# Block sums of the FFN up-projection: built per pair in SBUF instead of ahead in DRAM

## The reference

```python
def conv_ffn(h, p):
    u = dwconv(h @ p['w_up'], p['ffn_conv']) + p['ffn_conv_b']
    val, gate = jnp.split(u, 2, axis=-1)
    return (val * jax.nn.silu(gate)) @ p['w_down']
...
        h2 = rmsnorm_2(h_res, g_ffn_pre[l])
        up = centred_dwconv(h2 @ w_up[l], conv_w_ffn[l], conv_b_ffn[l])
        a, v = jnp.split(up, 2, axis=-1)
        ffn_out = (jax.nn.gelu(a) * v) @ w_down[l]
        h_res = h_res + rmsnorm_2(ffn_out, g_ffn_post[l])
```

## Time and profile before

| | |
|---|---|
| three runs | 3824.38, 3827.13, 3827.26 us, median 3827.13 |
| profiled execution, and its span | 3828.93 us, 3827.1 us |
| PE, PE weight loads busy | 3424.5 (89%), 3114.0 (81%) |
| DVE, ACT, POOL busy | 2276.1 (59%), 1580.3 (41%), 234.1 (6%) |
| DMA queues: q1 (SP and others), q0 (POOL) | 332.72 MB, 28.5%; 191.47 MB, 17.2% |

### The profile page before, as it was taken

The page is one execution under the profiler, slowest core; times in us unless marked ns, Lnnn a source line. Parts: engine busy times, 40 slices in busy tenths (PEclk is TensorE's granted clock), DMA queues, the critical chain, the costliest instruction groups (busy, mean ns, idle before and its releaser), DMA issues.

```text
span 3827.1 us, 72929 instructions
## 1 busy us (share of the span) xinstructions
PE 3424.5 (89%) x30711; PEld 3114.0 (81%) x30711; DVE 2276.1 (59%) x3617; ACT 1580.3 (41%) x2735; POOL 234.1 (6%) x399
## 2 busy tenths in 40 slices
PE   8999978867798989889999996499999999999999
PEld 4787778867787778667788996379999989999999
DVE  5477756756575764776776883122223577777576
ACT  4566633333234764533344552111113443334454
POOL 2000000000000000000000112100000000000110
PEclk9999989888898999999999998699999999999999
DMA  6244455457523305333345766961113333344675
GB/s 234 74 143 136 142 201 185 162 126 175 136 64 77 80 29 145 97 108 110 114 136 186 264 214 232 253 133 38 45 50 91 117 103 111 108 140 122 240 243 163
DMA packets 396766, 528.85 MB, mean 138 GB/s; under 512 B 20596, under 2 KB 311895, under 8 KB 392345
## 3 DMA queue, kind: packets, MB, share of 16 engines
q1 hardware_dynamic: 353160, 332.72, 28.5%
q0 software_dynamic: 43280, 191.47, 17.2%
HBM read 441.17 MB, written 175.21 MB: 161 GB/s over the span
## 4 chain that ended last, share of the span: by engine, by line
PE 45%; DVE 6%; issue 3%; DMA 3%; ACT 2%; another core or an unknown queue 2%; DVEq 2%; ACTq 0%; POOL 0%
PE psum L3587 8%; PE psum L3588 7%; PE psum L3589 7%; PE psum L2849 4%; PE psum L2850 4%; PE psum L2851 4%; PE psum L2370 3%; PE psum L2372 3%; PE psum L2371 3%; DMA down_w_raw<-in_w_down 1%; DMA down_w_raw<-in_w_in 1%; DVE mix_u_val L3877 1%; DVE mix_u_gate L3877 1%; PE psum L3488 1%
## 5 line engine op out<-in xcount | busy, mean ns | idle before, releaser
L2236 DVE TENSOR_TENSOR down_w_lo<-down_w_raw,down_w_hi 128x1024 fp32r<-128x1024 f32 x228 | 270.5, 1187 | 562.2 <-ACT down_w_hi L2210 559.9
L2210 ACT ACTIVATE down_w_hi<-down_w_raw 128x1024 fp32r<-128x1024 f32 x228 | 234.7, 1029 | 695.5 <-PE psum L2851 283.5
L3434 DVE TENSOR_TENSOR mix_w_split<-mix_w_raw,mix_w_split 128x512 fp32r<-128x512 f32 x372 | 255.4, 688 | 296.1 <-ACT mix_w_split L3430 295.8
L2370 PE MATMUL psum<-down_ghi,down_w_hi 128*128 128x256 f32 x1408 | 404.1, 287 | 11.7 <-DVE down_glo L2241 11.5
L2372 PE MATMUL psum<-down_glo,down_w_hi 128*128 128x256 f32 x1408 | 399.5, 284 | 0.0
L2371 PE MATMUL psum<-down_ghi,down_w_lo 128*128 128x256 f32 x1408 | 399.2, 284 | 0.0
L3587 PE MATMUL psum<-mix_t_hi,mix_w_split 128*128 128x258 f32 (+1 forms) x1056 | 339.9, 322 | 13.7 <-DVE mix_t_lo L3815 13.6
L3588 PE MATMUL psum<-mix_t_hi,mix_w_split 128*128 128x258 f32 (+1 forms) x1056 | 339.3, 321 | 0.0
L3589 PE MATMUL psum<-mix_t_lo,mix_w_split 128*128 128x258 f32 (+1 forms) x1056 | 339.0, 321 | 0.0
L2849 PE MATMUL psum<-h_hi,down_w_hi 128*128 128x348 f32 (+2 forms) x768 | 254.1, 331 | 74.1 <-DVE down_w_lo L2236 35.8
L3430 ACT ACTIVATE mix_w_split<-mix_w_raw 128x512 fp32r<-128x512 f32 x372 | 228.0, 624 | 155.7 <-PE psum L3589 134.4
(11 more groups left out here) (499 smaller groups left out, 8537.1 us busy)
## 6 DMA issues: line engine op xcount, KB each, us to landing
down_w_raw<-in_w_down SPq DMA_DIRECT2D x176, 512.0 KB, 4.3
up_sums<-in_w_up POOLq DMA_DIRECT2D x48, 1408.0 KB, 20.1
mix_w_raw<-up_sums SPq DMA_DIRECT2D x176, 256.0 KB, 2.9
mix_w_raw<-in_w_up SPq DMA_DIRECT2D x132, 256.0 KB, 3.1
up_sums<-up_sums POOLq DMA_DIRECT2D x16, 1408.0 KB, 24.6
g_scratch<-mix_u_val POOLq DMA_DIRECT2D x44, 512.0 KB, 3.6
down_w_raw<-in_w_in SPq DMA_DIRECT2D x36, 512.0 KB, 4.0
down_g_part<-g_scratch POOLq DMA_DIRECT2D x6, 2816.0 KB, 16.6
```

The costliest lines, as they stand in the source:

```text
L2210: self.nc.scalar.activation(self.hi[s][:, 0:w], self.raw[s][:, 0:w], ACT.Copy).then_inc(self.w_high, 1)
L2236: last = self.nc.vector.tensor_tensor(self.lo[s][:, 0:w], self.raw[s][:, 0:w], self.hi[s][:, 0:w].bitcast(F32), ALU.subtract)
L2370: nc.tensor.matmul(out, w_hi[:, w], g_hi[:, :], start=(n == 0 and c % 2 == 0), stop=False, skip_group_check=True)
L3434: nc.vector.tensor_tensor(ring[s % 4][:, 1, :], raw[s % RAWS][:, :], ring[s % 4][:, 0, :].bitcast(F32), ALU.subtract).then_inc(w_low.sem, 1)
```

## The change

`sum_weights`, its calls and the tensor `up_sums` are gone. SP loads 5 tiles per pair in the late steps (A11, S1, S3, A12, A22, where S1 and S3 start as their first block). POOL adds the second block into each of S1 and S3 by an accumulating transfer from `w_up` into the SBUF tile (`add_blocks`, L3489 in the new numbering), two pairs ahead; its rows are 512 bytes. DVE makes the other two sums in place: `first_sum` adds S1 to A11 (for P6, L3471), and a second add puts A11 on A12 (for P3, L3463). ACT's high parts of P6 and P3 wait for these adds. In the order of steps, P3 of an early pair changes places with P1 of the pair behind it, where that pair is not early (7 times in each mixer). The norms' chain of the first half (a = 0) takes the form that the second half had, both run a step sooner, and one more `low_turns` stands ahead of the late steps.

```diff
-                sum_weights(pool, k, 0, i)
...
-        for i in range(32):
-            sum_weights(pool, self.k, 1, i)
...
+    for at in range(len(late) - 1):
+        if late[at][0] == "P3" and late[at][1] in EARLY and late[at + 1][0] == "P1":
+            late[at:at + 2] = late[at + 1], late[at]
...
+    tiles += [(what, i, "late") for i in range(KF) for what in ("A11", "S1", "S3", "A12", "A22")]
+    SOURCE = {"P1": "A11", "P6": "A11", "P7": "S3", "P5": "S1", "P2": "A12", "P3": "A12", "P4": "A22"}
...
+        if kind == "P6":
+            act.wait_ge(*w_added.at(2 * i + 1))
+        elif kind == "P3":
+            act.wait_ge(*w_added.at(2 * i + 2))
...
     def weight_low(dve, s):
...
+        if s + 1 < STEPS and steps[s + 1][0] == "P6":
+            first_sum(dve, steps[s + 1][1])
+        elif kind == ("P5" if i in EARLY else "P2") and s >= first_late:
+            dve.drain()
+            a11, a12 = (raw[tile_of[what, i, "late"] % RAWS] for what in ("A11", "A12"))
+            wait_landed(dve, tile_of["A12", i, "late"])
+            nc.vector.tensor_tensor(a12[:, :], a12[:, :], a11[:, :], ALU.add).then_inc(w_added.sem, 1)
+
+    def first_sum(dve, i):
+        t11, ts1 = tile_of["A11", i, "late"], tile_of["S1", i, "late"]
+        wait_landed(dve, t11)
+        wait_landed(dve, ts1)
+        dve.drain()
+        a11, s1 = raw[t11 % RAWS], raw[ts1 % RAWS]
+        nc.vector.tensor_tensor(a11[:, :], a11[:, :], s1[:, :], ALU.add).then_inc(w_added.sem, 1)
...
+    def add_blocks(pool, i):
+        for what, added in (("S1", "A22"), ("S3", "A11")):
+            t = tile_of[what, i, "late"]
+            slot = t % RAWS
+            pool.wait_ge(*w_landed[slot].at(landed_at(t)))
+            pool.dma_start(raw[slot][:, :].rearrange("p (k n) -> p k n", n=P), block(added, i),
+                           accum_op=ALU.add).then_inc(blocks_added[i % 2].sem, 16)
...
         def chain(a, e):
             if e == 1:
                 means(a, 0)
-            elif a == 1:
-                if 3 <= e <= 6:
-                    residual(a, 2 * e - 6, 2 * e - 5)
-                elif e == 8:
-                    means(a, 1)
...
+            elif 2 <= e <= 5:
+                residual(a, 2 * e - 4, 2 * e - 3)
+            elif e == 7:
                 means(a, 1)
```

More of the change, by code:

```diff
@@ L3321, in mixer_out_to_ffn @@
     w_up = spec["w_up"].rearrange("(k p) n -> p k n", p=P)
-    w_sums = [k.up_sums[spec["mixer"]][j].rearrange("(k p) n -> p k n", p=P) for j in range(4)]
     UNITS = 2 * KD
@@ L3329, in mixer_out_to_ffn @@
     first_late = 2 * UNITS + 2 * QUEUE
-    late_at = {i: min(s for s in range(first_late, STEPS) if steps[s][1] == i) for i in range(KF)}
+    late_at = {i: index["P3", i - 1] + 1 if i else first_late for i in range(KF)}
     RAWS = 10
-    landed_at = lambda s: 16 * (s // RAWS) + 16
+    tiles = [(*st, "all") for st in steps[:2 * UNITS]] + [(*steps[s], "early") for s in range(2 * UNITS, first_late)]
+    tiles += [(what, i, "late") for i in range(KF) for what in ("A11", "S1", "S3", "A12", "A22")]
+    TILES = len(tiles)
+    tile_of = {tile: t for t, tile in enumerate(tiles)}
+    landed_at = lambda t: 16 * (t // RAWS + 1)
+    SOURCE = {"P1": "A11", "P6": "A11", "P7": "S3", "P5": "S1", "P2": "A12", "P3": "A12", "P4": "A22"}
     chain_of = lambda s: (s // (2 * KD) - 1, s % (2 * KD)) if 2 * KD <= s < 6 * KD else (None, None)
@@ L3410, in mixer_out_to_ffn, with source, block, tile @@
     up.first_took = max(u[1] for u in upper if u[0] == "took")
-    up.raw_free = [max(s + 1 for s in range(STEPS) if s % RAWS // 2 == j) for j in range(2)]
     after.up = up
-    def source(s):
-        kind, i = steps[s][0:2]
-        if kind == "O":
-            h = steps[s][2]
-            return w_out[:, 4 * h:4 * h + 4, i % KD * P:i % KD * P + P]
-        if kind in SUMS:
-            return w_sums[SUMS.index(kind)][:, :, i * P:i * P + P]
-        c = (i + side[0 if kind == "P4" else 1]) * P
-        return w_up[:, 0:4, c:c + P] if kind == "P1" else w_up[:, 4:8, c:c + P]
-    def weight_high(act, s):
-        act.wait_ge(*w_landed[s % RAWS].at(landed_at(s)))
+    def source(t):
+        what, i = tiles[t][0:2]
+        if what == "O":
+            h = tiles[t][2]
+            return w_out[:, 4 * h:4 * h + 4, i % KD * P:i % KD * P + P]
+        return block(what, i)
+    def block(what, i):
+        low, c = {"A11": (0, 1), "P1": (0, 1), "A12": (4, 1), "P2": (4, 1), "A22": (4, 0), "S1": (0, 0), "S3": (0, 0)}[what]
+        c = (i + side[c]) * P
+        return w_up[:, low:low + 4, c:c + P]
+    def tile(s):
+        kind, i = steps[s][0:2]
+        return s if s < first_late else tile_of[SOURCE[kind], i, "late"]
+    def wait_released(eng, t):
+        what, i = tiles[t][0:2]
+        if t < first_late:
+            eng.wait_ge(*w_low.at(t + 1))
+        elif what == "A11":
+            eng.wait_ge(*w_added.at(2 * i + 2))
+        else:
+            eng.wait_ge(*w_low.at(index[{"S1": "P5", "S3": "P7", "A12": "P3", "A22": "P4"}[what], i] + 1))
+    def wait_raw(eng, j):
+        for slot in (2 * j, 2 * j + 1):
+            wait_released(eng, max(range(slot, TILES, RAWS)))
+    def wait_landed(eng, t):
+        what, i = tiles[t][0:2]
+        if what in BY_DMA:
+            eng.wait_ge(*blocks_added[i % 2].at(32 * (i // 2 + 1)))
+        else:
+            eng.wait_ge(*w_landed[t % RAWS].at(landed_at(t)))
+    up.wait_raw = wait_raw
+    def weight_high(act, s):
+        kind, i = steps[s][0:2]
+        t = tile(s)
+        if kind == "P6":
+            act.wait_ge(*w_added.at(2 * i + 1))
+        elif kind == "P3":
+            act.wait_ge(*w_added.at(2 * i + 2))
+        else:
+            wait_landed(act, t)
         if s >= 4:
@@ L3435, in weight_low @@
                                 ALU.subtract).then_inc(w_low.sem, 1)
-    def sync(sp):
-        for s in range(STEPS):
-            if s >= RAWS:
-                sp.wait_ge(*w_low.at(s - RAWS + 1))
-            elif before and s < 4:
-                sp.wait_ge(before.low, before.total - 1 + s // 2)
+        if s + 1 < STEPS and steps[s + 1][0] == "P6":
[5 more added lines that the diff above has]
+            nc.vector.tensor_tensor(a12[:, :], a12[:, :], a11[:, :], ALU.add).then_inc(w_added.sem, 1)
@@ new lines, in first_sum @@
+    def first_sum(dve, i):
[5 more added lines that the diff above has]
+        nc.vector.tensor_tensor(a11[:, :], a11[:, :], s1[:, :], ALU.add).then_inc(w_added.sem, 1)
+    def sync(sp):
+        for t in range(TILES):
+            if t >= RAWS:
+                wait_released(sp, t - RAWS)
+            elif before and t < 4:
+                sp.wait_ge(before.low, before.total - 1 + t // 2)
@@ L3466, in gpsimd @@
             pool.wait_ge(*x_stored[a].at(16 * KD))
+        for i in range(2):
+            add_blocks(pool, i)
         for m in range(KF):
+            if m + 2 < KF:
+                add_blocks(pool, m + 2)
             pool.wait_ge(*g_ready.at(m + 1))
@@ L3927, in vector @@
                 chain(a, e)
[L3928 to L3929 removed]
+            if first_late <= s < first_late + 3:
+                low_turns(TURNS[2 + s - first_late])
             if s >= first_late:
```

128 lines of the change are left out of this document (38 added, 90 removed).

## The result

The changed kernel takes 3635.4 us (median of four runs, 3630.13 to 3644.34) against 3827.2 us before: the ratio is 0.950, with a 95% interval of 0.948 to 0.952. The forecast was 3642. The total came out nearly as the sum said, but two of its three terms were wrong, in opposite directions: the scan gave 41 us more than forecast, the mixers cost 23 us more. That the total is within 7 us is luck in part.

What follows compares the result with a forecast made beforehand. Bounds: the sums' DMA traffic delaying loads in scan and merge stage; PE, with DVE short of slack, in the mixers' late steps. From 3828.9 us, -82 (scan), -111 (merge), +6 (mixers), 0 (added transfers) gave 3642; range 3600 to 3700.

Steps and rivals of the forecast that it cites:

- The merge stage, -111: Merge stage: without the sums' DMA traffic pieces of w_in land quickly and PE is the bound, -111 us.
- The scan, -82: RWKV scan: PE's waits for h go, its clock rises, the first unit starts sooner, -82 us.
- The mixers, +6: Both mixers: adds on DVE's path cost time, shorter chains give some back, +6 us in all.
- (a): Late steps, two-pair cycles: DVE's path becomes 39.9 us; six cycles cost 5.4 us in mixer 0, 7.8 in mixer 1.
- (b): Late steps, pairs 14 to 21: DVE's path becomes 20.3 to 20.4 us a pair, costing 6.4 and 2.4 us.
- (c): Ahead of the late steps: the shorter chain has low_turns done sooner, gaining 9.9 and 7.0 us.
- The added transfers, 0: Mixers: accumulating transfers at 0.055 us a row land in 4 to 6 us, hidden by POOL's lead, 0 us.
- Rival 3: Added transfers: an accumulating row costs a fixed time whatever its length, some +600 us, 4250; chance 0.08.
- Rival 1: Scan: unit loads and mod_w alone keep the DMA late, only -25 us there, 3699; chance 0.15.
- Rival 2: Mixers: DVE takes the adds inside its waits and the swap frees PE, cycles of 33.6 us, 3558; chance 0.07.
- Rival 4: Merge stage: another wait replaces DMA's, half the gain, 3698; chance 0.05.
- Rival 5: Mixers: DVE's adds and POOL's issue of accumulating transfers block each other, +60 us, 3702; chance 0.03.

Runs made afterwards that it cites:

- before_no_merge_sums: Kernel before with mixer 1's 32 transfers of block sums left out (mixer 1 reads mixer 0's sums): 3723.1 us, -109 against 3831.8.
- scan_sums: Changed kernel with the 32 transfers of mixer 0's sums put back between the mod_w loads in the RWKV scan: 3732.2 us, +97.
- no_adds: Changed kernel without DVE's 88 adds of 128x512, their drains and waits kept: 3578.0 us, -57.
- early_sum: Changed kernel with P3 and P1 exchanged wherever P1 follows P3, and non-early pairs' first sum one step sooner: 3627.6 us, -8.
- high_first: Changed kernel with ACT making the high part four steps ahead before it centres, at P4 and P3: 3536.6 us, ratio 0.923 to the kernel before.
- pool_adds: Changed kernel with both adds of each pair on GpSimd in place of DVE: 3766.2 us, +131.

## Why the prediction was right in its total and wrong in two terms

**The merge stage, -111: right.** It measured -109.9 in the change and in before_no_merge_sums. The step-by-step sum of PE's own work, with no allowance for loads, was the right method, since nothing else was near its limit there.

**The scan, -82: the mechanism right, two terms too small.** Idle time fell by 91 us where 76 (73.3 - 5, and 8 for the first unit) were forecast; the 73.3 us of the earlier trace rows cover 560 to 1042, and the scan runs from 495.5 to 1122.8, with a first wait of 11.4 us that they leave out. The larger miss was the clock: "so I take a third, 8" of the 25 us. It measured 32 us of busy time with the same matmuls. The 25 were themselves taken from 382 of the 504 us that PE is busy in the scan; by the same formula the whole of it gives 504.3 x (1 - 0.87 / 0.93) = 33, and 42 for the 0.95 that was reached. So three quarters of what the clock could give came, not a third. The reason I gave, that small matmuls in a chain wait on latency, largely counts that twice: their waits for other engines stand in the idle time already. scan_sums shows the two parts coming back together.

**The mixers, +6: three terms off by 23 in all, +29 measured.** Ahead of the late steps the chains gave 7.8 and 4.6 us, so the late steps themselves cost 22.0 and 19.6. (a) DVE's path in cycles of two pairs: "28.4 + 7.6 + 4 x 0.78 = 39.1", taken as 39.9, measured 40.4; with mixer 1's base of 38.3, not 38.6, and seven cycles, not six, that is 10.1 and 15.1 us instead of 5.4 and 7.8. no_adds shows which part was wrong. The adds are cheaper than the sum has them, 0.60 us against 0.78, and the path without them is longer: 37.9 against 28.4 + 7.6 = 36.0. Of these 1.9 us the timeline shows 0.6, two waits of 0.31 us for ACT in a cycle; the rest was not traced. (b) Pairs 14 to 21: forecast 20.3 to 20.4, measured 21.1 to 21.5, so over six periods 9.8 and 6.0 us in place of 6.4 and 2.4. (18.7 and two adds of 0.78 make 20.2 already, so hardly any of the margin named in the sum is in it.) In the timeline stands a new wait of 0.70 us behind the first sum, yet early_sum, made to remove it, brought back 0.3 to 0.4. The list of what is queued behind the added instruction was made for DVE, but not for what ACT does between the sum and the low part. (c) The chains gave 7.8 and 4.6 us instead of 9.9 and 7.0, of which mixer 1's is inside the scatter of the profiles.

**The added transfers, 0: right.** Neither ACT nor DVE waits for a transfer in the changed kernel's late steps, and high_first ran its late steps in 400.7 us with the same transfers at a DMA share of 0.62. They landed in 7.0 us (median of the page) where 4 to 6 were estimated, and a row took 0.232 x 16 x 12 us / 708 = 0.063 us (row below) where 0.055 was taken. Rival 3's price of 0.29 and more for a row isn't there for rows of 512 bytes. (Its 4250 was too high by its own numbers: 22 cycles of 24 us more give 528, or 4170.)

```profile
q0 software_dynamic: 708, 0.35, 23.2%
```

(queue q0 of high_first, 1800 to 1812, when it held accumulating transfers).

**The rivals.** Rival 1 fell: unit loads land in 5.6 us with `mod_w` still beside them. Rival 2 (PE the bound, the adds inside DVE's waits) fell for this change, but is nearly what high_first makes: its total of 3558 was named for cycles of 33.6 us, high_first has 34.9. The argument against it, the round trip of 1.83 us, was the right one, and the step that I didn't take was to ask whether that trip must be so. Rival 4 fell: PE is busy 100 of 100 us in the merge stage's window. Rival 5 fell: the adds took 691 to 696 ns in the changed kernel. The Trainium skill's rule ("SBUF — State Buffer", section on who interferes with whom) doesn't reach POOL's issue of DMAs in this trace: 61 low parts and 37 of the first sums ran while POOL issued accumulating transfers, and took 680 to 694 and 691 to 696 ns as elsewhere (no tap ran beside an issue). Where GpSimd itself computes from SBUF, pool_adds agrees with the rule: 2.40 us for a tap of 1.28.

## What to carry to other kernels

Bulk work that is hidden on an idle queue can be paid for by whoever loads small pieces beside it, as in the scan and the merge stage here: read a stage's DMA share together with the waits of its loads, and price the stage without it by PE's own instructions, with all of its busy time scaled by the clock (three quarters of that came in the scan). An engine that is busy 75% of the time (DVE, 150.2 of 200 us) can still be the bound when its order of instructions goes through another engine: lay out the path from take to next take on paper, and look for the instruction that could be issued sooner (a move of two instructions on ACT gave 99 us here, half as much as the whole change). When an instruction is added on such a path, count its own time and also who answers it: the add cost 0.6 us, and the answer stood as 0.7 in the timeline.
